# A two-block model on one core: the order of work ahead of and around the Fourier mixer

## The reference

```python
sh1x, sc1x, g1x, sh2x, sc2x, g2x = adaln_params(c, ada_w[0], ada_b[0])      # silu(c) @ w + b, six rows of 1024
sh1c, sc1c, g1c, sh2c, sc2c, g2c = adaln_params(c_ctx, ada_w[0], ada_b[0])
hx = rmsnorm(x, norm_g[0, 0]) * (1.0 + sc1x) + sh1x
x = x + g1x * (real(fft2(hx, over tokens and 4 groups of 256 channels)) @ w_o + b_o)
hc = rmsnorm(ctx, norm_g[0, 0]) * (1.0 + sc1c) + sh1c
ctx = ctx + g1c * (the same of hc)
hx = rmsnorm(x, norm_g[0, 1]) * (1.0 + sc2x) + sh2x
x = x + g2x * ec_moe(hx, ...)                                               # 16 experts, each takes its best tokens
```

## Time and profile before

| | us |
|---|---|
| median of 3 runs | 3818.35 |
| the profiled execution | 3827.83 |
| its span, first to last instruction | 3826.0 |
| TensorE busy in the span | 3626.3 (95%) |
| VectorE busy | 1574.6 (41%) |
| ScalarE busy | 802.6 (21%) |
| GpSimd busy | 730.7 (19%) |
| first Fourier product starts | 89.50 |
| stage 2 starts | 108.40 |
| stage 3 starts | 125.68 |
| first expert product starts | 229.44 |

### The profile page before, as it was taken

One profiled execution on the slowest core, in us unless ns is written; L12 is line 12 of the kernel. 1 busy time (PEld: TensorE's weight loads), 2 busy tenths in 40 slices (PEclk: granted clock), 3 DMA queues, 4 the chain that ended last, 5 costly groups with the idle time before them and its releaser, 6 DMA issues.

```text
span 3826.0 us, 84150 instructions
## 1 busy us (share of the span) xinstructions
PE 3626.3 (95%) x35394; PEld 2267.6 (59%) x35394; DVE 1574.6 (41%) x3428; ACT 802.6 (21%) x1807; POOL 730.7 (19%) x644
## 2 busy tenths in 40 slices
PE   5999999999989898899999999999999999999998
PEld 4544444455557777764344344455888744558887
DVE  1421111164466666653122133742545437425454
ACT  1210010020145555541000011061000010610000
POOL 3200000000034434420000000002343300023433
PEclk8999999999999999999999999999999999999999
DMA  9399999942300000012999981101222211012221
GB/s 378 126 397 375 376 391 362 392 203 78 116 11 13 14 18 17 14 54 112 424 428 429 428 361 45 66 24 44 89 88 88 97 45 66 24 44 89 88 89 44
DMA packets 56483, 626.44 MB, mean 164 GB/s; under 512 B 5920, under 2 KB 9248, under 8 KB 20640
## 3 DMA queue, kind: packets, MB, share of 16 engines
q1 hardware_dynamic: 49808, 599.68, 39.2%
q0 software_dynamic: 3968, 14.16, 1.3%
q10 hardware_dynamic: 2448, 8.91, 0.6%
HBM read 604.64 MB, written 18.09 MB: 163 GB/s over the span
## 4 chain that ended last, share of the span: by engine, by line
PE 84%; DVE 6%; DMA 3%; issue 3%; ACT 2%; DVEq 1%; ACTq 1%; SPq 0%
PE bank L987 68%; PE bank L1540 11%; DMA work<-slabs 3%; PE bank L1922 1%; PE bank L1935 1%; PE bank L1595 1%; DVE hx L2721 1%; PE bank L1015 1%; DMA ring<-slabs 1%; DVE work L2697 1%; ACTq L2601 0%; ACT work L2600 0%; DVE work L2706 0%; DVE work L3121 0%; PE bank L1403 0%
## 5 line engine op out<-in xcount | busy, mean ns | idle before, releaser
L987 PE MATMUL bank<-work 128*64 128x512 f32 (+10 forms) x5142 | 855.2, 426 | 14.6 <-issue 5.2
L987 PEld LDWEIGHTS bank<-work 128*64 128x64 f32 (+5 forms) x5142 | 493.5, 153 | 347.3 <-issue 267.6
L987 PE MATMUL bank<-ring,work 128*64 128x512 f32 (+4 forms) x4506 | 498.4, 436 | 53.2 <-DMA ring<-slabs 44.6
L987 PE MATMUL bank<-hx,ring 128*128 128x512 f32 (+1 forms) x1344 | 483.8, 516 | 5.1 <-DVE hx L2721 2.8
L987 PE MATMUL bank<-work,ring 128*128 128x256 f32 (+1 forms) x1616 | 481.3, 457 | 6.6 <-DVE work L3062 3.4
L987 PEld LDWEIGHTS bank<-work,ring 128*128 128x128 f32 x1616 | 307.5, 191 | 173.9 <-issue 133.3
L987 PEld LDWEIGHTS bank<-ring,work 128*32 128x32 f32 (+3 forms) x4506 | 210.7, 126 | 326.0 <-issue 272.2
L987 PEld LDWEIGHTS bank<-hx,ring 128*128 128x128 f32 x1344 | 256.2, 192 | 220.5 <-issue 200.4
L3757 POOL TENSOR_TENSOR work<-ring 128x512 f32<-128x512 f32 (+1 forms) x44 | 69.3, 1576 | 1565.5 <-ACT work L2148 1167.8
L2697 DVE TENSOR_TENSOR work<-work,bank 128x256 f32<-128x256 f32 x240 | 91.9, 416 | 384.3 <-ACT work L2675 380.8
L1540 PE MATMUL bank<-work 64*64 64x64 f32 x9216 | 193.3, 225 | 32.3 <-issue 20.4
(11 more groups left out here) (390 smaller groups left out, 4547.7 us busy)
## 6 DMA issues: line engine op xcount, KB each, us to landing
ring<-slabs SPq DMA_DIRECT2D x177, 2048.0 KB, 10.8
work<-slabs SPq DMA_DIRECT2D x82, 2048.0 KB, 15.5
hx<-slabs SPq DMA_DIRECT2D x17, 2048.0 KB, 10.0
work<-kv SPq DMA_DIRECT2D x18, 384.0 KB, 3.1
kv<-work SPq DMA_DIRECT2D x2, 3072.0 KB, 15.6
kv<-work ACTq DMA_DIRECT2D x6, 512.0 KB, 6.3
resx<-xT SPq DMA_DIRECT2D x1, 2048.0 KB, 11.4
kv<-work POOLq DMA_DIRECT2D x1, 2048.0 KB, 29.5
```

The lines of the kernel that those rows point to most:

```text
L987: return pe.matmul(out, lhsT, rhs, start=(k == 0), stop=(k == n - 1))
```

## The change

The slabs are stored and loaded in a new order, `FRONT`: six slabs of the modulation, the two of out-weights, four of the modulation, the tables, the last two of the modulation. The tables `C` and `S` (514 columns, "waves") are loaded a second time, by a transfer of their own ahead of all slabs.

On TensorE the sums of squares come first, before any slab. They are half as long in products, as tiles k and k + 4 of the squares are added first: x's squares by ScalarE, their addition and all of the context's by VectorE. Then come four modulation slabs with two unused products between each (`kept_warm(P[0], 2)`), the transposes of these four, and pass 1 of stage 1. Slabs 4 and 5 are multiplied between the passes, 6 to 9 between stages 1 and 2, and 10 and 11 between stages 2 and 3. The modulation is turned and biased in three groups of four slabs (`ada_turned(g)`, `modulation(g)`). ScalarE copies the products out, not VectorE. Six unused products are put at the very start.

VectorE multiplies x by the root and folds it; GpSimd does so only for the context, then the out-weights, then `w128`. `wide_router` is multiplied after stage 2. The loads wait for what used each slab: those that follow an out-weights slab for GpSimd's `norm_pool`. Last, the 12 unused products before the first experts become 4.

```diff
+AD_PE = [("sums",)] + [(_n, _g) for _g in range(3) for _n in ("summed", "turned")]
+AD_DVE = [("context",)] + [("added", _k) for _k in range(4)] + [("folded",)] + [("mod", _g) for _g in range(3)]
+AD_ACT = [("copied", _g) for _g in range(3)]
+FRONT = ["a0", "a1", "a2", "a3", "a4", "a5", "w0", "w1", "a6", "a7", "a8", "a9", "tables", "a10", "a11"]
...
+            sp.dma_start(waves, slabs_d[FRONT.index("tables")][:, 0:FN["S"][1]]).then_inc(waves_loaded, 16)
...
-            single(0, ADA_SLABS, 0)
             f0 = ADA_SLABS + FNET_SLABS
+            used = 0
+            for n in range(f0 - RING):
+                if FRONT[n] in ("w0", "w1"):
+                    sp.wait_ge(norm_pool, 2 + int(FRONT[n][1]))
+                else:
+                    used += 1
+                    sp.wait_ge(slab_used, used)
+                load(n + RING)
             sp.wait_ge(*rt_done("pe", "shift"))
             load_first(f0 + RING, f0 + RING)
-            single(ADA_SLABS, f0, 0)
+            sp.wait_ge(norm_pool, 4)
+            for n in range(f0 - RING, f0):
+                used += 1
+                sp.wait_ge(slab_used, used)
+                load(n + RING)
...
+            kept_warm(P[0], 6)
...
+            def ada_turned(g):
+
+                pe.wait_ge(*ad_done("act", "copied", g))
+                if g:
+                    pe.wait_ge(*ad_done("dve", "mod", g - 1))
+                for q in range(4):
+                    m = pe.transpose(P[6][:, 128 * q:128 * q + 128], adarow[:, (4 * g + q) * 128:(4 * g + q + 1) * 128], ident)
+                m.then_inc(ad_pe, ad.one("turned", g))
...
+            pe.wait_ge(*ad_done("dve", "context"))
+            for k in range(4):
+                mm(P[5][:, 0:NC], ones, sqc0[:, k, :], k, 4)
+            for k in range(4):
+                pe.wait_ge(*ad_done("dve", "added", k))
+                m = mm(P[4][:, :], ones, sqx0[:, k, :], k, 4)
...
+            for n in range(4):
                 ada_slab(n)
+                if n < 3:
+                    kept_warm(P[0], 2)
+            ada_turned(0)
...
                     m.then_inc(filled, me.add("filled"))
+                for n in (4, 5) if pair == 0 else ():
+                    ada_slab(n)
+            me.t["slab"].n += 2
+            ada_slab(6)
+            ada_slab(7)
             pe.wait_ge(fed, me.next("fed"))
+            ada_turned(1)
+            ada_slab(8)
+            ada_slab(9)
+            pe.wait_ge(slab_loaded[me.slot()], me.landed())
+            tables = flat(me.next_slab())
...
-                kept_warm(P[1], 12)
+                kept_warm(P[1], 4)
...
+            v.wait_ge(norm_act, KT + 1)
+            tt(ux, resx[:, :, :], bc(rstd[:, 0:NX].unsqueeze(1), 128, KT, NX), ALU.mult)
+            v.drain()
+            half = NX // 2
+            near, far = ux[:, :, 1:half], ux[:, :, NX - 1:half:-1]
+            tt(hx[:, :, 1:half], near, far, ALU.add)
+            tt(hx[:, :, half + 1:NX], near, far, ALU.subtract)
...
-            for res, u, n, at in ((resx, ux, NX, 0), (resc, uc, NC, NX)):
-                pool.tensor_tensor(u, res[:, :, :], rstd[:, at:at + n].unsqueeze(1).to_broadcast([128, KT, n]), ALU.mult)
+            pool.tensor_tensor(uc, resc[:, :, :], rstd[:, NX:NX + NC].unsqueeze(1).to_broadcast([128, KT, NC]), ALU.mult)
             pool.drain()
```

More of the change, by code:

```diff
@@ L1093, in late_rows_turned @@
                 m.then_inc(late_turned, 1)
-            for n in range(RING):
-                ada_slab(n)
[L1097 to L1119, removed]
+            pe.wait_ge(*ad_done("dve", "context"))
[4 more added lines that the diff above has]
+                m = mm(P[4][:, :], ones, sqx0[:, k, :], k, 4)
+            m.then_inc(ad_pe, ad.one("sums"))
+            me.t["na"].n += 1 + 2 * KT
+            me.t["nd"].n += KT
+            pe.wait_ge(answered, 1)
+            pe.wait_ge(fed, me.next("fed"))
+            for n in range(4):
+                ada_slab(n)
+                if n < 3:
+                    kept_warm(P[0], 2)
+            ada_turned(0)
+            me.first_bank()
+            me.width = 6
+            pe.wait_ge(waves_loaded, 16)
             def fn(name, a=None, n=None):
                 lo, hi = FN[name]
-                return wf[:, lo:hi] if a is None else wf[:, lo + a * n:lo + (a + 1) * n]
+                whole = waves if name in "CS" else tables
+                return whole[:, lo:hi] if a is None else whole[:, lo + a * n:lo + (a + 1) * n]
             for pair in range(2):
@@ L2179, in _, with ada_copied @@
             act.preload_act_table_set("natural_log_exp_and_others")
[L2180 to L2183, removed]
+            ad = Steps(AD_ACT)
+            def ada_copied(g):
+                act.wait_ge(*ad_done("pe", "summed", g))
+                act.activation(adarow[:, 512 * g:512 * g + 512], P[7][:, :], ACT.Copy).then_inc(ad_act, ad.one("copied", g))
+            act.wait_ge(x_loaded, 16)
+            for k in range(4):
+                for half in range(2):
+                    tile_square(k + 4 * half, [(resx, sqx0)], wait=False)
+            act.wait_ge(*ad_done("pe", "sums"))
+            for at, b, n in ((0, P[4], NX), (NX, P[5], NC)):
+                act.activation(rstd[:, at:at + n], b[:, 0:n], ACT.Ln, bias=tiny, scale=1.0 / D)
+            act.drain()
+            act.activation(rstd[:, :], rstd[:, :], ACT.Exp, scale=-0.5).then_inc(norm_act, me.add("na"))
+            ada_copied(0)
+            act.wait_ge(*ad_done("dve", "mod", 0))
             for k in range(KT):
@@ L2744, in _ @@
[L2744 to L2752 removed]
+            ad = Steps(AD_DVE)
@@ new lines, in _ @@
+            v.wait_ge(context_loaded, 16)
+            tt(sqc0, resc[:, :, :], resc[:, :, :], ALU.mult)
+            v.drain()
+            v.tensor_tensor(sqc0[:, 0:4, :], sqc0[:, 0:4, :], sqc0[:, 4:8, :], ALU.add).then_inc(ad_dve, ad.one("context"))
+            for k in range(4):
+                v.wait_ge(norm_act, 2 * k + 2)
+                v.tensor_tensor(sqx0[:, k, :], sqx0[:, k, :], sqx0[:, k + 4, :], ALU.add).then_inc(ad_dve, ad.one("added", k))
+            v.wait_ge(norm_act, KT + 1)
@@ L2782, in _ @@
             v.drain().then_inc(fed, me.add("fed"))
+            modulation(1)
+            tt(gate_bias, bc(vec("fnet_bo").unsqueeze(2), 128, KT, 2), mod[:, 0, 2, :, :], ALU.mult)
+            v.tensor_scalar(ngate, mod[:, 0, 2, :, :], -1.0, None, ALU.mult).then_inc(ad_dve, ad.one("mod", 1))
+            v.drain().then_inc(asked, me.add("asked"))
+            rt = Steps(RT_DVE)
+            v.memset(wide_router[:, :, :, :], 0.0)
             me.first_bank()
@@ L2793, in _ @@
             v.tensor_copy(less_shift, P[5][0:NE, 0:2]).then_inc(rt_dve, rt.one("shift"))
+            modulation(2)
+            gained(1).then_inc(ad_dve, ad.one("mod", 2))
+            v.drain()
+            for j in range(2):
+                m = v.tensor_tensor(wide_router[:, j, :, 0:NE], router[:, 0, :, :], bc(mod[:, 0, 4, :, j:j + 1], 128, KT, NE), ALU.mult)
+            m.then_inc(rt_dve, rt.one("router"))
             me.first_bank()
```

123 lines of the change are left out of this document (62 added, 61 removed).

## The result

The changed kernel takes 3833.61 us (median of 6 runs, 3829.32 to 3838.97) against 3818.06 for the kernel before (6 runs): 15.5 us slower, ratio 1.0041, 95% interval 1.0029 to 1.0052. The prediction was 3812.7, with 3801 to 3820 as its range. Measured again later, with five more runs of the changed kernel beside 13 of the kernel before, it was 3836.03 and the ratio 1.0036 (1.0023 to 1.0050).

A forecast was written before the change was run, and what follows sets the result against it. The front was taken as bound by loads up to 89.5 us, then by TensorE to 125.7. Gains of 2.3 (front) and 3.3 (unused products) sum to 5.6 us: 3818.35 - 5.6 = 3812.7, range 3801 to 3820.

The forecast's parts named there:

- That a start that comes earlier is kept: Experts: TensorE is busy 99.75 of 100 us at full clock, so an earlier start there shortens the whole.
- anything behind the experts' start changes its length: Sign of a wrong prediction: work after the experts' start was to keep its length.
- Sums and root: Front, before the fold: sums of squares end at 26.8 us, the root 2.0 us later at 28.8.
- The fold, taking turns: VectorE and GpSimd alternate by instruction: 9.4 plus 9.2 us, fold ends at 47.4, first Fourier product at 49.4.
- The first rival: Folds hardly block each other: first Fourier product at 42.9, all behind it 6.5 us earlier, 3806.2 us; chance 0.22.
- Pass 1, the gap in the loads, the tables: Stage 1 to stage 2: first pass 10.8 us, transfers still for some 13 us, tables landed at 99.1.
- It starts after waits, and I add 2.5 us for the clock (0 to 3.4): Stage 2: 16.6 us as before plus 2.5 for a lowered clock, ending at 118.2.
- my 123.4: Start of stage 3, after slabs 10 and 11, router's product, copy and transposes; 125.7 before, so 2.3 us gained.
- The second rival: Clock decides: TensorE's short work after waits runs at half level, kernel gets slower, +7.7 us, 3826.0; chance 0.11.
- The unused products: Before the first experts: 4 instead of 12 save 4.3 us, less 1.0 for the clock, gain 3.3.

The follow-up runs named there:

- early: Changed kernel with four unused products before the tables, plus slabs 4 and 5 multiplied ahead of the first pass of stage 1: 3806.32 us, ratio 0.9960 to the kernel before.
- fill: Changed kernel with four unused products of 512 columns between slab 9 and the tables, ahead of stage 2: 3813.85 us, ratio 0.9986 to the kernel before.
- best4: Changed kernel with fillers before the tables, slabs 4 and 5 ahead of stage 1, all folding on VectorE, 4 unused products before the experts: 3810.75 us, ratio 0.9975.
- alldve: Changed kernel with four unused products before the tables, and the context folded by VectorE instead of GpSimd: 3810.11 us, ratio 0.9973 to the kernel before.
- changed: The changed kernel measured again, unaltered, with a second profile: 3836.03 us, ratio 1.0036 to the kernel before.
- oldwait: The kernel before, with GpSimd repeating one sum of out-weights and TensorE made to wait for it ahead of stage 2: 3844.08 us, ratio 1.0062.
- mid: Changed kernel with six unused products inside stage 2, after the first of its four groups, none before it: 3823.38 us, ratio 1.0007 to the kernel before.
- four: The kernel before with only the 12 unused products ahead of the first experts cut to 4: 3821.84 us, ratio 1.0009.

## Why the prediction was wrong

Point by point, by its own steps:

- *That a start that comes earlier is kept.* Only in part. `early` keeps its 15.5 us at the first expert as 13.7 in the median, but `fill` keeps 5.3 of 9.9 and `best4` 9.8 of 17.5, and the changed kernel, 3.2 late there, is 15.5 late at the end. I had also said that the prediction is wrong if anything behind the experts' start changes its length, and it did.
- *Sums and root.* Right: 26.4 and 28.4 where 26.8 and 28.8 were worked out.
- *The fold, taking turns.* Right, and shown by `alldve`: x's fold ended at 46.0 for 47.4, the first product came at 47.85 for 49.4. The rule of the Trainium skill ("SBUF — State Buffer", section "SBUF: two separate sides") that spoke against this part of the change holds here, with 13.03 us beside 4.57 for the same operations. The first rival (side by side) is out. (Its 42.9 should have been 43.2 by its own terms.)
- *Pass 1, the gap in the loads, the tables.* Right in kind: 9.9 us of a first pass for 10.8, no loads from about 50 to 60 where I had a gap of 13 us, the tables at 95.9 for 99.1. `early` shows the gap's price, 7 us.
- *"It starts after waits, and I add 2.5 us for the clock (0 to 3.4)".* This step failed. I took the longest fall of the clock that I had rows for, one followed by products of another kind (the sums, which brought it back), and put it on stage 2. There the clock was down from 2 us into stage 2 to about the end of slab 10, 30.7 us in the first profile of the changed kernel, and for 34.1 us in `changed`, from before stage 2 on. Measured at the place: 34.87 us for stage 2 and both slabs against the 23.1 that I summed, so 11.8 more. The tables came 3.2 us early, so stage 3 starts 8.6 us after my 123.4. `fill` takes 19.8 us back by four products at this one place: the step was the mistake, and `oldwait` and `mid` show its mechanism on both sides.
- *The second rival* named the clock as the way to slower, but priced stage 2 and both slabs together at +1.6 over the forecast. Its price was off by 10 us there.
- *The unused products.* From stage 3 to the first expert some of it came (3.2 and 1.5 us in the two profiles of the changed kernel, 2.3 in `four`), but not in the whole: instead of 3.3 us faster, `four` is 2.7 slower, within an interval that reaches 0. The gathered rows' landing is not a fixed moment, and the clock falls in the wait.

That `fill` ends at 3813.85, 1.2 us from the forecast, is in part luck: stage 3 starts 5.1 us earlier than in the kernel before, not 2.3, the first expert 9.9 and not 5.6, and some of that is lost behind.

What stays open: the miss is 20.9 us (3833.61 for 3812.7), and only 8.8 of them stand at the first expert (232.6 for 223.8). The other 12 came behind it. `fill` shows that part of them hangs on the same place (of the 20 to 22 us between it and the changed kernel, 11.5 lie before stage 3 and 13 before the first expert in the two profiles), but not how. The mean clock of all timed runs points the same way (0.983 and 0.982 against 0.988). Each profile has short falls of the clock behind 240 us. Some stand at the same place in all of them (near 790 to 830 and 2480 to 2550), others do not, and together they last 61 and 52 us in the two profiles of the changed kernel, 54 in those of `fill` and of the kernel before, and 34 in that of `oldwait`. The profile of the kernel before is of a slow execution, so this does not say how much of the 12 us they make. What divides the kernels better is the number of unused products. From the first expert to the end (median less the landmark, against the kernel before of the same group) the four other kernels with 12 take 1 to 2.5 us more than the kernel before, and the eight measurements with 4 take 2 to 12 us more. The landmarks are of one execution each, that of the kernel before 9.8 us above its median, so this is a hint and no proof. Nor was it tried what in stage 2's products (20 of its 74 records work on two rows, and all fill about half a bank or less) keeps them from raising the clock.

## What to carry to other kernels

When a reordering makes TensorE wait just ahead of a long stage, look at the stage's products, not only at the length of the wait: a stage can run at half clock from end to end though TensorE is never idle in it, and a stretch that is busy at a clock of 0.50 is the sign of it. A few unused dense products in the wait can cost more than they cover (here 3.9 us in a wait of 1.75) and still be worth it: they gave 20 us. Don't split one chain of two-input operations between VectorE and GpSimd: all of it on VectorE was ready 3.8 us sooner. And free a ring's slots before a long stage, not behind its first part. Last, read a gain or a loss from the medians as well as from landmarks of one profile; here they differ by up to 12 us.

## What the runs showed of the hardware

- The granted clock stayed at the lower level for 41.0 us on end in `oldwait` (from 108.1 us), with TensorE idle to 112.7 and busy from then on, and went back to the upper one in stage 3's dense products. After six dense products in `mid` the same stage ran at the upper level to its end.
- VectorE and GpSimd changed places after every instruction, both ways: 8.77 us for an operation of 4.54 behind one of 4.43, and 13.03 us for three of 4.57 in all.
